# Last layer's last row tile turned unscaled, first expert's rows by one-hot products, the other lists made inside its up product

## What is computed

```python
def _rmsnorm(x, g):
    y = xf * lax.rsqrt(jnp.mean(xf * xf, axis=-1, keepdims=True) + NORM_EPS)
    return (y * g.astype(jnp.float32)).astype(x.dtype)
...
def _moe(h, router, w1, w3, w2):
    logits = jnp.einsum('btd,de->bte', h, router).astype(jnp.float32)
    top_v, top_i = lax.top_k(logits, TOP_K)
    gates = jax.nn.softmax(top_v, axis=-1)
...
    for e in range(N_EXP):
        y = y + combine[..., e:e + 1] * _swiglu(h, w1[e], w3[e], w2[e])
```

## Time and profile before

| | us |
|---|---|
| median of 3 runs | 1876.15 |
| lowest, highest run | 1874.99, 1879.84 |
| span of the profiled execution, first to last instruction | 1869.9 |
| what the median run has around that span | 6.25 |
| layer 1's experts, from the first up product (977.77) to the end of the span | 892.1 |

### The profile page before, as it was taken

The page is one execution under the profiler, slowest core; times in us unless marked ns, Lnnn a source line. Parts: engine busy times, 40 slices in busy tenths (PEclk is TensorE's granted clock), DMA queues, the critical chain, the costliest instruction groups (busy, mean ns, idle before and its releaser), DMA issues.

```text
span 1869.9 us, 38456 instructions
## 1 busy us (share of the span) xinstructions
PE 1808.4 (97%) x17710; PEld 981.9 (53%) x17710; DVE 470.3 (25%) x1039; ACT 249.2 (13%) x570; POOL 91.3 (5%) x118
## 2 busy tenths in 40 slices
PE   8999899999999999989989999999999999999997
PEld 6778875666666677887562333333333333333332
DVE  2436655200000343565641001001100100110031
ACT  2342222100000234222210000000000000000001
POOL 0000012100000000001310000000000000000000
PEclk9999897999999899989879999999999999999999
DMA  7330012723330433001199999999999999999992
GB/s 244 102 105 3 3 66 65 302 113 136 133 125 1 131 101 106 2 3 67 65 362 379 396 407 411 409 421 414 407 414 402 422 402 421 415 409 415 413 415 96
DMA packets 66663, 453.62 MB, mean 243 GB/s; under 512 B 10208, under 2 KB 37152, under 8 KB 42048
## 3 DMA queue, kind: packets, MB, share of 16 engines
q1 hardware_dynamic: 60704, 431.43, 57.6%
q0 software_dynamic: 5376, 19.49, 2.8%
q10 hardware_dynamic: 416, 0.16, 0.0%
HBM read 441.47 MB, written 9.60 MB: 241 GB/s over the span
## 4 chain that ended last, share of the span: by engine, by line
PE 93%; DVE 5%; ACT 1%; issue 1%; DMA 0%; DVEq 0%; SPq 0%; ACTq 0%
PE bank L541 91%; PE bank L545 2%; DVE ring L1373 1%; DVE work L1373 1%; DVE hT L1373 1%; DMA X<-x_in_dram 0%; DVE X L1373 0%; DVE work L1376 0%; DVE hT L1776 0%; DVE AV L1708 0%; ACT ring L2315 0%; DVE hT L1800 0%; ACT work L2339 0%; ACT L2228 0%; ACT L2318 0%
## 5 line engine op out<-in xcount | busy, mean ns | idle before, releaser
L541 PE MATMUL bank<-ring,hT 128*32 128x512 f32 (+2 forms) x6336 | 626.3, 538 | 0.7 <-DVE hT L1373 0.7
L541 PEld LDWEIGHTS bank<-ring,hT 128*32 128x32 f32 (+1 forms) x6336 | 223.5, 112 | 401.3 <-issue 388.3
L541 PE MATMUL bank<-hT,ring 128*128 128x288 f32 x1632 | 408.7, 411 | 2.4 <-DVEq L1426 2.4
L541 PE MATMUL bank<-ring,work 128*32 128x512 f32 (+4 forms) x3168 | 390.8, 569 | 0.0
L541 PEld LDWEIGHTS bank<-hT,ring 128*128 128x128 f32 x1632 | 311.3, 192 | 100.6 <-issue 13.8
L1373 DVE TENSOR_TENSOR work<-work,bank 128x384 f32<-128x384 f32 (+2 forms) x142 | 78.1, 560 | 766.1 <-ACT work L2460 502.7
L541 PEld LDWEIGHTS bank<-ring,work 128*32 128x32 f32 (+3 forms) x3168 | 129.5, 116 | 238.4 <-issue 235.3
L2460 ACT ACTIVATE work<-bank 128x512 f32<-128x512 f32 (+1 forms) x48 | 26.1, 544 | 549.9 <-PE bank L541 549.9
L541 PE MATMUL bank<-ring 64*64 64x64 f32 (+11 forms) x1152 | 78.3, 287 | 5.3 <-DVE SS L1373 2.7
L2224 ACT ACTIVATE ring<-bank 128x32 f32<-128x32 f32 (+7 forms) x144 | 41.5, 335 | 193.2 <-PE bank L541 168.6
L541 PEld LDWEIGHTS bank<-ring 64*64 64x64 f32 (+6 forms) x1152 | 54.9, 146 | 20.0 <-issue 13.0
(11 more groups left out here) (257 smaller groups left out, 1026.5 us busy)
## 6 DMA issues: line engine op xcount, KB each, us to landing
ring<-moe_dram SPq DMA_DIRECT2D x168, 2048.0 KB, 10.8
ring<-ffn_dram SPq DMA_DIRECT2D x22, 1536.0 KB, 12.7
ring<-w_in_dram SPq DMA_DIRECT2D x18, 1536.0 KB, 6.5
ring<-w_out_dram SPq DMA_DIRECT2D x2, 1536.0 KB, 7.3
work<-w_out_dram SPq DMA_DIRECT2D x2, 1280.0 KB, 7.8
ring<-w_out_dram SPq DMA_DIRECT2D x2, 1280.0 KB, 10.4
ring<-w_in_dram SPq DMA_DIRECT2D x2, 1152.0 KB, 5.3
C<-consts_dram SPq DMA_DIRECT2D x1, 1912.5 KB, 16.0
```

The source lines that it names most:

```text
L541: return nc.tensor.matmul(out, lhsT, rhs, start=start, stop=stop, skip_group_check=True)
```

## The change

There are four edits, all in layer 1.

- The last tile is turned from `X`, not scaled, in two halves of four transposes (`row_transposes`, DVE's `rows_turned`). The logits of a row are scaled by that row's reciprocal root when DVE copies them. On PE the first half's transposes and the short tile's logits are put between the third and the fourth of the eight k of the tile's last out product.
- The logits lie in two fills (tiles 2 and 0; tile 1), and the totals have a fill of their own behind the slots.
- The first expert's rows come from products of `hn` with the one-hot (`first_rows`, 24 products of 128 x 96) instead of list, gather and transposes.
- The lists of the other seven experts (21 products) are made on PE after the first of the eight k of the first expert's first half. SP's wait on the first gathered rows is gone.

```diff
+            def row_transposes(l, part):
+
+                last = ORDER[1][2]
+                wait(pe, out_ok, l, 1 + part)
+                b, full = fill(pe, l, "hT", 5, part)
+                for q in range(4):
+                    k = part * 4 + q
+                    i = tr(pe, b[:, q * P:(q + 1) * P], X[:, last, k * P:(k + 1) * P])
+                i.then_inc(full, 1)
...
+                bank, full = fill(pe, l, "out", 1, 2)
+                out_products(l, 1, 2, bank, first)
+                row_transposes(l, 0)
+                early = fill(pe, l, "logits", 0)
+                logits(l, early[0], 0, 0)
+                logits(l, early[0], 0, 1)
+                out_products(l, 1, 2, bank, rest).then_inc(full, 1)
+                return early
...
-                b, full = fill(pe, l, "logits")
-                logits(l, b, 0)
-                logits(l, b, 1)
-                norm_transposes(l, 1, 2)
-                logits(l, b, 2).then_inc(full, 1)
+            def routing(l, early):
+                logits(l, early[0], 1, 0)
+                row_transposes(l, 1)
+                logits(l, early[0], 1, 1).then_inc(early[1], 1)
+                b, full = fill(pe, l, "logits", 1)
+                logits(l, b, 2, 0)
+                logits(l, b, 2, 1).then_inc(full, 1)
...
+                i.then_inc(full, 1)
+                b, full = fill(pe, l, "totals")
                 for t, (t0, n) in enumerate(TILES):
-                    i = mm(pe, b[:, 3 * N_EXP:4 * N_EXP], cst("ones", rows=n), small[0:n, 1, t, :], start=t == 0, stop=t == 2)
+                    i = mm(pe, b[0:32, 0:N_EXP], cst("ones", 0, 32, rows=n), small[0:n, 1, t, :], start=t == 0, stop=t == 2)
...
+            def first_rows():
+
+                wait(pe, hn_ok, DEPTH - 1, 5)
+                wait(pe, hn_half_ok, DEPTH - 1, 0)
+                pe.wait_ge(hot_ok, 3)
+                for part in range(2):
+                    for q in range(4):
+                        k = 4 * part + q
                         for t, (t0, n) in enumerate(TILES):
+                            i = mm(pe, banks[Y_BANKS[part]][:, q * CAP:(q + 1) * CAP], hn_at(1, t)[0:n, k * P:(k + 1) * P], hot[0:n, t, 0, :],
+                                   start=t == 0, stop=t == 2)
+                    i.then_inc(turned, 1)
...
                 for k in range(KD):
+                    if k == KD // 2 and not half and job == 0:
+                        pe.wait_ge(hG_ok, 2)
+                    if k == 1 and not half and job % N_EXP == 0:
+                        later_lists(job // N_EXP)
...
             def start_round(r):
-                if r:
-                    pe.wait_ge(tail_added, 3)
-                slot_lists(r)
+                if r == 0:
+                    first_rows()
+                    return
...
+                if l:
+                    rows_turned(l, 1)
                 wait(dve, rstd_ok, l, 5)
                 V.tensor_scalar(hn_at(1, last)[:, D // 2:], X[:, last, D // 2:], stat[:, last, 2:3], None, MUL).then_inc(hn_half_ok.sem, 1)
-                transposed(l, 1, 2)
+                if l == 0:
+                    transposed(l, 1, 2)
...
-                    if job == 0 and q == FIRST_STEPS[OPEN_STEPS + 1]:
-                        sp.wait_ge(xg_loaded, 16)
```

More of the change, by code:

```diff
@@ L333, in trunk @@
         hid_e = part(work, hidden_at, GROUPS, 512)
+        last_rows = part(work, 21 * NT, KD, P)
         hid_t = part(work, hidden_at + GROUPS * 512, D_EXP // FB, CAP)
@@ L1089, in out_projection, with logits @@
                 norm_transposes(l, 1, 1)
-                whole(1, 2)
-            def logits(l, bank, at):
+                if l == 0:
+                    whole(1, 2)
+                    return
[7 more added lines that the diff above has]
+                return early
+            def logits(l, bank, at, part):
                 t = ORDER[1][at]
                 t0, n = TILES[t]
[L1095 to L1098, removed]
-                return i
-            def routing(l):
-                b, full = fill(pe, l, "logits")
-                logits(l, b, 0)
-                logits(l, b, 1)
-                norm_transposes(l, 1, 2)
-                logits(l, b, 2).then_inc(full, 1)
+                wait(pe, hT_ok, l, 6 + 2 * at + part)
+                for k in range(4 * part, 4 * part + 4):
+                    rows = last_rows[:, k, :] if at == 2 else hT[:, k, t0:t0 + n]
+                    i = mm(pe, bank[0:n, t * N_EXP:(t + 1) * N_EXP], rows, rt_w[:, k, :], start=k == 0, stop=k == KD - 1)
+                return i
+            def routing(l, early):
[5 more added lines that the diff above has]
+                logits(l, b, 2, 1).then_inc(full, 1)
                 wait(pe, chosen_ok, 0, 0)
@@ L1344, in _ @@
                 means(l, RW_K)
-                out_projection(l)
+                early = out_projection(l)
                 if l == 0:
@@ L1350, in _ @@
                 else:
-                    routing(l)
+                    routing(l, early)
                     for b in range(8):
@@ L1417, in norm, with rows_turned @@
                 dve.wait_ge(inputs, 32)
+            def rows_turned(l, part):
+                b, free = take(dve, l, "hT", 5, part)
+                tt(last_rows[:, 4 * part:4 * part + 4, :], b[:, :].rearrange("p (a b) -> p a b", a=4), over(par(l, "ln_ffn", 4 * part, 4), P, 2), MUL)\
+                    .then_inc(free, 1)
+                freed(dve, l, "hT", 5, part)
+                V.engine_nop().then_inc(hT_ok.sem, 1)
             def transposed(l, use, at):
@@ L1860, in norm_outputs @@
                 inverted(2)
+                if l:
+                    rows_turned(l, 1)
                 wait(dve, rstd_ok, l, 5)
                 V.tensor_scalar(hn_at(1, last)[:, D // 2:], X[:, last, D // 2:], stat[:, last, 2:3], None, MUL).then_inc(hn_half_ok.sem, 1)
-                transposed(l, 1, 2)
+                if l == 0:
+                    transposed(l, 1, 2)
             def routing(l):
[L1867 to L1870, removed]
+                b, free = take(dve, l, "logits", 0)
+                own(V.tensor_copy(small[:, 0, 0, :], b[:, 0:N_EXP]))
+                V.tensor_copy(small[0:32, 0, 2, :], b[0:32, 2 * N_EXP:3 * N_EXP]).then_inc(free, 1)
+                b, free = take(dve, l, "logits", 1)
+                last = ORDER[1][2]
+                V.tensor_scalar(small[:, 0, last, :], b[:, last * N_EXP:(last + 1) * N_EXP], stat[:, last, 2:3], None, MUL).then_inc(free, 1)
+                for at in range(2):
+                    freed(dve, l, "logits", at)
                 settle()
@@ L2049, in take_turned @@
                     w = par(1, "ln_ffn", 4 * part, 4)
[L2050 removed]
+                    bank = banks[3 + part] if job else banks[Y_BANKS[part]]
+                    tt(hG[:, 4 * part:4 * part + 4, :], bank[:, 0:4 * CAP].rearrange("p (a b) -> p a b", a=4),
                        over(w, CAP, 2), MUL).then_inc(hG_ok, 1)
```

76 lines of the change are left out of this document (48 added, 28 removed).

## The result

| | before | with the change |
|---|---|---|
| median, us (18 runs each, taken side by side) | 1878.73 (1871.96 to 1884.77) | 1884.03 (1876.41 to 1892.68) |
| ratio, 95% interval | | 1.0033 [1.002, 1.0046] |
| span of the profiled execution, mean granted clock | 1869.9, 0.968 | 1887.9, 0.960 |

The change costs 5.3 us, where the prediction had +1.65. The three runs shown with the kernel before had a median of 1876.15; the runs beside the change have 1878.73, so 2.6 of the distance between 1877.8 and 1884.03 is a shift of the base, and 3.65 is the error of the sum. The interval lies wholly above 1, so the loss is real, though it is no larger than the 5.6 us that the prediction called the limit of a measurement.

What follows compares the result with a forecast made beforehand. PE was taken as the bound, its up product's start set by a chain of small steps and PE's clock. -4.55 + 4.2 + 2.0 = +1.65 us gave a median of 1877.8, range 1871.5 to 1882.5.

Steps and rivals of the forecast that it cites:

- logits read earlier: Router chain: DVE reads the logits at about 954.8 instead of 956.99, -2.2 us.
- first PE work on one-hots: After logits and totals: starts at 961.6 instead of 964.98, from terms of -2.2 and -1.15 us.
- up product's start: First expert's up product starts at 973.2 instead of 977.77, -4.55 us, the shorter chain included.
- step 0: Weight load issued at about 950.9, landing at 968.7, 4.5 us ahead of the up product at 973.2.
- First expert by one-hot products: Ahead of the up product: 48 PE instructions at half clock take 11.6 us, bounds 6.0 to 12.3.
- Other lists inside the up product: First expert's up product: 42 list instructions delay it one for one, at full clock, +4.2 us.
- The clock behind the lists: Up product after the lists: they may drop PE's clock again, bounds 0 and 4, middle taken, +2.0 us.
- Half clock at the up product's start: First 4.0 us of the up product at half clock cost 2.0 as before, so a change of 0.
- the one-hot products did not lift the clock: Denies the rival that these products raise PE's clock before the up product: 1872.1 or 1870.1 us, chance 0.28.
- The lists at half clock: Rival: PE's clock is 0.50 at the first list inside the up product, time 1884.8 us, chance 0.09.
- The early fall: Rival: PE's clock falls before the logits end, +3.2 us, about 1881; chance 0.08 shared with a late weight load.
- the late step 0: Rival: first weight load lands a few us late behind other traffic, about 1881; chance 0.08 shared with early clock fall.

Runs made afterwards that it cites:

- products by tile: The change with the one-hot products ordered tile after tile within each half of k (rows not the reference's); 0.9999 of the kernel before, median -0.6 us.
- Lists spread, picks first: The change with one expert's list behind each of k 1 to 7, DVE casting them after its picks and token rows; 1.0018 of the kernel before, +3.0 us.
- filled: The change plus unread products of constants on PE, three behind the last logits, two behind the totals; 0.9991 of the kernel before, median -1.9 us.
- falls in the other: Unread constant products in PE's two router waits, added to the change with lists in pieces and cast late; 0.9983 of the kernel before, -2.3 us.
- chain only: Only the first two edits (unscaled turn; logits and totals in own fills), the other two undone; 0.9982 of the kernel before, median -2.9 us.
- rows and lists only: Only the last two edits (first expert's rows by one-hot products, lists inside the up product); 1.0044 of the kernel before, median +9.8 us.
- lists spread: The change with one expert's list behind each of k 1 to 7, DVE's cast still ahead of its picks; 1.0042 of the kernel before, +7.6 us.

## Why the prediction was wrong, by its own steps

| step | predicted | measured |
|---|---|---|
| logits read earlier | -2.2 | -2.66 (966.44 - 12.11 = 954.33, for 956.99) |
| first PE work on one-hots | -3.35 in all | -3.83 (961.15, for 964.98) |
| one-hot products | 11.6 | 14.18 |
| up product's start | -4.55 | -2.52 |
| half clock at its start | 0 | +0.45 |
| lists inside it | +4.2 | +5.27 |
| second fall of the clock | +2.0 | +2.78 |
| sum | +1.65 | +6.0 (stage +6.06, median +5.3) |

The mechanism held at nearly every step: transposes and logits at full clock, products at half, step 0 landed (980.86) ahead of the up product (987.36), lists at full clock until 999.0, a second fall, no stop for loads. The sizes failed, three of them in the same direction.

*First expert by one-hot products* is the step that was off most, by 2.6. It bounded the products from above at 12.3, eight times the totals' six of 1.54, as "the same mix". The mix of rows was the same, but those products stream 8 columns and these 96. The starts of the totals' six lie 0.235, 0.213, 0.213, 0.291 and 0.235 apart: going to the 32-row tile costs 0.12 there, and they never come back from it. Here going and coming back costs 0.49, eight times ("products by tile"). So the real value lay beyond the bound that I called the top, and the -4.55 came out as -2.52 although the chain ahead of it gave half a microsecond more than forecast.

*Other lists inside the up product* took full clock to be "about half" of 8.00 "by the ratio of the streams above". But that ratio is 0.125 to 0.208, or 0.60, and 0.60 of 8.00 is 4.8: a slip that the prediction's own figures show. "Lists spread, picks first" has a piece of six in 0.68 (990.48 - 989.80), 0.113 an instruction: 4.76 for 42. The other 0.5 is the lists' end, which ran after the clock had fallen at 999.0. The prediction had such a fall inside the lists as its upper bound, and its middle value left it out.

*The clock behind the lists* was taken at the middle of 0 and 4 and came out at 2.78 behind the lists, 3.41 with what was lost inside them.

*Half clock at the up product's start* was taken to be as before. The +0.45 is within the 2.61 to 4.84 us in which the clock rose in these kernels, so it is no property of the change that the runs show.

The rivals: the one-hot products did not lift the clock. PEclk is 0.50 from 968.4 to 992.1, with PE busy without a stop in the last 18.8 us of it, 14.18 of them these products. The Trainium skill ("TensorE: Matmul & The Clock Gate", Part 1, What's actually happening) says that sustained activity releases the clock; this trace does not agree for the 14.18 us of products that load 128 columns and stream 96. The lists at half clock (1884.8) landed nearest by its time, but not by its mechanism: the lists began at 1.00. The early fall and the late step 0 did not occur.

The range was too narrow above, since it took the middle of two unknown costs and left no room for the base; with products at 14.2 and the fall at 4, its own sum is 1882.4, and the base moved by 2.6. What the prediction never asked was what its own terms say of the two halves. The chain's are -2.2 - 1.15 = -3.35. The other half's are -1.2 (11.6 for the 12.8 of list, gather and turning), +4.2 and +2.0, a loss of 5.0: by its own sum the chain alone was the better kernel. Measured, the halves are -4.51 and +9.79. The prediction knew that the old wait was full of the lists and charged them again in their new place, which is right; that they had already cost 4 us in the old one, so that gather and turning were not worth 12.8, it did not read from the rows.

**Still open.** Why the clock stays at 1.00 through the one-hot products in one filled kernel and falls in the other. Why a block of lists drops the clock and pieces do not: the traces show that it is so, not by what. Whether chain only gains from filler. Products by tile with sums of the reference, a first expert turned ahead of the other lists, and a gather that does not wait for the `hn_rows` stores, were not tried.

## What to carry to other kernels

Work that fills a wait is free only for the part that the wait covers: look for the end of what is waited for (here 971.33) inside the work (967.26 to 975.26). When a change removes the wait, put the work's whole time on the other side of the sum, at the clock of its new place, and give the block's effect on the clock a term of its own. Add up a prediction's terms for each half of a change, and cut the change into its halves early: here one half gains 4.5 us of the stage and the other loses 9.8, and the first half alone beats both kernels. Before moving a product on PE, look at what is queued on the engine that waits for its result.

## What was not expected of the hardware

- A detour from 128-row stationary tiles (the operand that is loaded) to a 32-row one and back cost 0.49 us at half clock with 96 streamed columns (14.18 for eight, 11.25 for two), on top of 0.213 from one product's start to the next.
- 42 products that load 96 columns and stream one, in one block that began at full clock, saw a fall to 0.50 inside the block in each of the four kernels that had them so (at 999.0 with the change, 992.4 by tile, 999.2 with rows and lists only, 991.2 filled). Cut into seven pieces of about 0.7 us between pieces of 5.4 us of up product, no fall came with them, in three kernels (the one at 1029.4 in "lists spread" came at the end of PE's wait for DVE).
- The granted clock's history differed between the two profiled executions even ahead of the edited work: for the same 8610 records PE was busy 890.66 us before and 904.27 with the change, at a mean granted clock of 0.95 and 0.94 (in 200 to 300, 0.82 and 0.76), and the stage began 12.1 us later.
